# The delta rule's triangular inverse on TensorE: 128x128 products at every level, or 64x64 products on the halves and one joining block

## The reference, cut to what matters

```
kk = jnp.einsum('bnhik,bnhjk->bnhij', k, k)
a_low = jnp.where(strict, kk * decay * beta[..., :, None], 0.0)
rhs = jnp.concatenate([v * beta[..., None], k * (beta * jnp.exp(gc))[..., None]], axis=-1)
uw = lax.linalg.triangular_solve(a_low + jnp.eye(C, dtype=a_low.dtype), rhs,
                                 left_side=True, lower=True, unit_diagonal=True)
...
    v_new = u_i - jnp.einsum('bhck,bhkv->bhcv', w_i, S)
    o_i = jnp.einsum('bhck,bhkv->bhcv', q_i, S) + jnp.einsum('bhij,bhjv->bhiv', qk_i, v_new)
    S = S * gl_i[..., None, None] + jnp.einsum('bhck,bhcv->bhkv', k_i, v_new)
```

## Time and profile before

| | us |
|---|---|
| median of 3 runs (lowest, highest) | 1306.34 (1304.51, 1308.42) |
| span of the profiled execution | 1308.6 |
| TensorE busy in it | 1204.4 |
| VectorE busy in it | 824.2 |
| ScalarE busy in it | 614.4 |
| delta stage's rounds 4 to 22 in it, about | 925 to 1082 |

### The profile page before, as it was taken

The page is one execution under the profiler, slowest core; times in us unless marked ns, Lnnn a source line. Parts: engine busy times, 40 slices in busy tenths (PEclk is TensorE's granted clock), DMA queues, the critical chain, the costliest instruction groups (busy, mean ns, idle before and its releaser), DMA issues.

```text
span 1308.6 us, 19807 instructions
## 1 busy us (share of the span) xinstructions
PE 1204.4 (92%) x8111; PEld 1070.4 (82%) x8111; DVE 824.2 (63%) x1298; ACT 614.4 (47%) x1097; POOL 63.9 (5%) x93
## 2 busy tenths in 40 slices
PE   2878999999999999889999999996789999999997
PEld 1757966788989889878999998995668887899996
DVE  7576574579998685557755447748665545544444
ACT  0431354564454455565455455365643334645543
POOL 0011055300000000000000000110000000000000
PEclk9989899999999999889999999898589999999999
DMA  9788502259999655323885651440000015456640
GB/s 351 277 294 297 196 28 65 97 181 350 365 348 339 218 167 171 116 78 118 284 272 184 215 181 37 135 153 1 1 1 17 1 65 177 134 190 192 193 162 33
DMA packets 138490, 218.76 MB, mean 167 GB/s; under 512 B 7056, under 2 KB 95504, under 8 KB 138016
## 3 DMA queue, kind: packets, MB, share of 16 engines
q1 hardware_dynamic: 138400, 217.49, 49.5%
HBM read 216.42 MB, written 1.05 MB: 166 GB/s over the span
## 4 chain that ended last, share of the span: by engine, by line
PE 78%; DVE 12%; ACT 5%; DMA 2%; issue 1%; POOL 1%; SPq 0%; DVEq 0%; ACTq 0%
PE bank L468 19%; PE bank L470 19%; PE bank L469 19%; PE bank L2146 2%; PE bank L2158 2%; PE bank L2154 2%; PE bank L493 2%; DVE ada_acc L537 1%; DMA ring<-ada_w 1%; PE bank L2406 1%; DMA ring<-ev_w_in 1%; DVE low L462 1%; DVE act_low L1335 1%; PE bank L1002 1%; PE bank L1037 1%
## 5 line engine op out<-in xcount | busy, mean ns | idle before, releaser
L462 DVE TENSOR_TENSOR low<-ring,high 128x2048 fp32r<-128x2048 f32 (+1 forms) x139 | 317.7, 2287 | 255.4 <-ACT high L456 254.8
L456 ACT ACTIVATE high<-ring 128x2048 fp32r<-128x2048 f32 (+1 forms) x139 | 264.5, 1905 | 262.0 <-PE bank L470 173.8
L468 PE MATMUL bank<-act_high,high 128*128 128x256 f32 (+1 forms) x1112 | 321.7, 289 | 6.0 <-DVE act_low L1335 6.0
L470 PE MATMUL bank<-act_high,low 128*128 128x256 f32 (+1 forms) x1112 | 316.4, 285 | 0.0
L469 PE MATMUL bank<-act_low,high 128*128 128x256 f32 (+1 forms) x1112 | 316.4, 285 | 0.0
L468 PE MATMUL bank<-high,act_high 128*128 128x512 f32 (+1 forms) x632 | 232.7, 368 | 2.5 <-DVE act_low L2651 1.8
L470 PE MATMUL bank<-high,act_low 128*128 128x512 f32 (+1 forms) x632 | 230.7, 365 | 0.0
L469 PE MATMUL bank<-low,act_high 128*128 128x512 f32 (+1 forms) x632 | 230.6, 365 | 0.0
L468 PEld LDWEIGHTS bank<-act_high,high 128*128 128x128 f32 x1112 | 214.0, 192 | 11.4 <-DVE act_low L1335 6.8
L469 PEld LDWEIGHTS bank<-act_low,high 128*128 128x128 f32 x1112 | 214.1, 193 | 2.6 <-issue 1.7
L470 PEld LDWEIGHTS bank<-act_high,low 128*128 128x128 f32 x1112 | 214.0, 192 | 0.0
(11 more groups left out here) (467 smaller groups left out, 1502.2 us busy)
## 6 DMA issues: line engine op xcount, KB each, us to landing
ring<-mlp_w SPq DMA_DIRECT2D x64, 1024.0 KB, 5.9
ring<-ada_w SPq DMA_DIRECT2D x48, 1024.0 KB, 7.2
ring<-w_up SPq DMA_DIRECT2D x16, 1024.0 KB, 5.6
ring<-w_down SPq DMA_DIRECT2D x16, 1024.0 KB, 4.9
ring<-od_w_in SPq DMA_DIRECT2D x12, 1024.0 KB, 5.2
ring<-w_in SPq DMA_DIRECT2D x11, 1024.0 KB, 5.3
ring<-ev_w_in SPq DMA_DIRECT2D x8, 1024.0 KB, 7.4
ring<-ev_w_out SPq DMA_DIRECT2D x4, 1024.0 KB, 8.3
```

The source lines that it names most:

```text
L456: e.activation(weights(c)[0], in_ring(("w", c)), ACT.Copy).then_inc(*act.up("high", c))
L462: e.tensor_tensor(low, in_ring(("w", c)), high.bitcast(F32), ALU.subtract).then_inc(*vec.up("low", c))
L468: e.matmul(out_, ah, bh, start=start, stop=False)
L470: return e.matmul(out_, al, bh, start=False, stop=stop)
```

## The change

For real chunks, X and XT of levels 0 to 5 are kept as their two 64x64 blocks on the diagonal, one on each half of the partitions, side by side in one buffer `xs` of eight groups (four heads of X, four of XT). A level's products are made as two 64x64 products a head, on the rows and columns of the array that belong to the half; X's and XT's updates go to one bank and are subtracted in one operation. At the level before the last, XT's blocks are written into a full 128x128 buffer, whose other corner was set to zero at the start. The last level makes the joining block alone: one 64x64 product a head from near rows to far columns, a copy, one product back, and a copy with a sign. Masks of the levels shrink to 64 columns, and one DMA of them with them. Meta chunks use the same buffers with their 16 rows whole. The order of steps, rounds and chunks is unchanged.

```diff
@@ square_masks
+    j = i // HALF * HALF + np.arange(HALF)[None, :]
     for back in (0, 1):
-        for level in range(LEVELS):
+        for level in range(JOIN):
...
+        def by_half(b, rows, n, at=0, groups=4):
+            return b[rows, at:at + groups * HALF].rearrange("p (g c) -> p g c", g=groups)[:, :, 0:n]
+
+        def halves_of(k, B, C, real, back):
+
+            if not real:
+                return (slice(0, C),), None, None, B["x"][0:C], B["w"][0:C, :, 0:C]
+            x = B["x"].rearrange("p a b -> p (a b)").rearrange("p (g c) -> p g c", g=8)
+            w = B["w"].rearrange("p a b -> p (a b)")[:, 0:4 * HALF].rearrange("p (g c) -> p g c", g=4)
+            return HALVES, HALVES[back], HALVES[1 - back], x, w
@@ delta_tensor
                 e.wait_ge(*vec.at("x", k, l - 1))
-                for h, o in enumerate(four(b)):
-                    m = e.matmul(o, B["aT"][0:C, h, 0:C], B["x"][0:C, h, 0:C], start=True, stop=True)
+                for h in range(4):
+                    if l == JOIN:
+                        m = e.matmul(b[far, at(h)], B["aT"][near, h, far], xs[near, h, :], start=True, stop=True)
+                    else:
+                        for r in parts:
+                            m = e.matmul(b[r, at(h)], B["aT"][r, h, r], xs[r, h, :], start=True, stop=True)
                 m.then_inc(*pe.up("w", k, l))
                 yield
                 e.wait_ge(*vec.at("w", k, l))
                 e.wait_ge(*vec.at("xT", k, l - 1))
-                if l < n_levels - 1:
-                    b = ps.take(e, ("x", k, l), vec, "x", k, l)
-                    for h, o in enumerate(four(b)):
-                        m = e.matmul(o, B["xT"][0:C, h, 0:C], B["w"][0:C, h, 0:C], start=True, stop=True)
-                    m.then_inc(*pe.up("x", k, l))
                 b = ps.take(e, ("xT", k, l), vec, "xT", k, l)
-                for h, o in enumerate(four(b)):
-                    m = e.matmul(o, B["w"][0:C, h, 0:C], B["xT"][0:C, h, 0:C], start=True, stop=True)
+                for h in range(4):
+                    if l == JOIN:
+                        m = e.matmul(b[near, at(h)], ws[far, h, :], B["xT"][far, h, far], start=True, stop=True)
+                        continue
+                    if l < n_levels - 1:
+                        for r in parts:
+                            e.matmul(b[r, at(h)], xs[r, 4 + h, :], ws[r, h, :], start=True, stop=True)
+                    for r in parts:
+                        m = e.matmul(b[r, at(4 + h)], ws[r, h, :], xs[r, 4 + h, :], start=True, stop=True)
                 m.then_inc(*pe.up("xT", k, l))
@@ delta_vector
-            e.tensor_tensor(v_("x"), v_("a"), level(0, 1 - back), ALU.mult).then_inc(*vec.up("x0", k))
+            for r in parts:
+                e.tensor_tensor(xs[r, 0:4, :], B["a"][r, :, r], level(0, 1 - back, r), ALU.mult).then_inc(*vec.up())
+            if real:
+                e.memset(B["xT"][far, :, near], 0.0).then_inc(*vec.up())
...
-            e.tensor_tensor(v_("xT"), v_("aT"), level(0, back), ALU.mult).then_inc(*vec.up("xT0", k))
+            for r in parts:
+                e.tensor_tensor(xs[r, 4:8, :], B["aT"][r, :, r], level(0, back, r), ALU.mult).then_inc(*vec.up())
+            vec.also("x0", k)
             e.wait_ge(*vec.at("x0", k))
-            e.tensor_tensor(v_("x"), idn, v_("x"), ALU.subtract).then_inc(*vec.up("x", k, 0))
-            e.wait_ge(*vec.at("xT0", k))
-            e.tensor_tensor(v_("xT"), idn, v_("xT"), ALU.subtract).then_inc(*vec.up("xT", k, 0))
+            e.tensor_tensor(xs, half_masks[0:C, 2 * JOIN, 0:N].unsqueeze(1).broadcast_to([C, 8, N]), xs, ALU.subtract).then_inc(
+                *vec.up("x", k, 0))
+            vec.also("xT", k, 0)
             for l in range(1, n_levels):
+                b = ps.of(("w", k, l))
                 e.wait_ge(*pe.at("w", k, l))
-                e.tensor_tensor(v_("w"), by_head(ps.of(("w", k, l)), C), level(l, 1 - back), ALU.mult).then_inc(*vec.up("w", k, l))
+                if l == JOIN:
+                    e.tensor_copy(ws[far], by_half(b, far, N)).then_inc(*vec.up("w", k, l))
+                else:
+                    e.tensor_tensor(ws, by_half(b, slice(0, C), N), level(l, 1 - back, slice(0, C)), ALU.mult).then_inc(*vec.up("w", k, l))
...
-                e.tensor_tensor(v_("xT"), v_("xT"), by_head(ps.of(("xT", k, l)), C), ALU.subtract).then_inc(*vec.up("xT", k, l))
+                if l == JOIN:
+                    e.tensor_scalar(B["xT"][near, :, far], by_half(b, near, N), -1.0, None, ALU.mult).then_inc(*vec.up("xT", k, l))
+                elif l == JOIN - 1:
+                    e.tensor_tensor(xs[near, 0:4, :], xs[near, 0:4, :], by_half(b, near, N), ALU.subtract).then_inc(*vec.up("x", k, l))
+                    for r in parts:
+                        e.tensor_tensor(B["xT"][r, :, r], xs[r, 4:8, :], by_half(b, r, N, 4 * HALF), ALU.subtract).then_inc(*vec.up())
+                    vec.also("xT", k, l)
+                elif l == n_levels - 1:
...
+                else:
+                    e.tensor_tensor(xs, xs, by_half(b, slice(0, C), N, 0, 8), ALU.subtract).then_inc(*vec.up("x", k, l))
+                    vec.also("xT", k, l)
@@ late_loads
-            e.dma_start(masks.rearrange("p a b -> p (a b)"), I["square_masks"][:, :]).then_inc(*landed.up("late"))
+            e.dma_start(all_masks, I["square_masks"][:, :]).then_inc(*landed.up("late"))
```

More of the change, by code:

```diff
@@ L47 @@
 LEVELS = 7
+JOIN = LEVELS - 1
 ALL = slice(0, SEQ)
@@ L79, in square_masks @@
     blocks = [*incl, *[np.where(m, 0.0, -NEG) for m in strict], *[np.where(m, 0.0, NEG) for m in incl]]
+    j = i // HALF * HALF + np.arange(HALF)[None, :]
     for back in (0, 1):
-        for level in range(LEVELS):
+        for level in range(JOIN):
             b = 1 << level
-            joined = (i // (2 * b) == j // (2 * b)) & (i // b % 2 == 0) & (j // b % 2 == 1)
-            blocks.append(joined.T if back else joined)
+            even, odd = (j, i) if back else (i, j)
+            blocks.append((i // (2 * b) == j // (2 * b)) & (even // b % 2 == 0) & (odd // b % 2 == 1))
+    blocks.append(i == j)
     return np.concatenate(blocks, 1).astype(np.float32)
@@ L359, in program @@
         LATE = 9
-        masks = mem.take("masks", 6 + 2 * LEVELS, P, at=late_at)
+        all_masks = mem.take("masks", 6 * P + (2 * JOIN + 1) * HALF, at=late_at)
+        masks = all_masks[:, 0:6 * P].rearrange("p (a b) -> p a b", a=6)
+        half_masks = all_masks[:, 6 * P:].rearrange("p (a b) -> p a b", a=2 * JOIN + 1)
         after = late_at + (6 + 2 * LEVELS) * P
@@ L1756, in program @@
         meta_bufs = [{**{n: mem.take(f"d{d}_{n}_meta", 4, META, at=early_at[d] + 3 * 512 + i * 64)
-                         for i, n in enumerate(("a", "aT", "x", "xT", "w"))},
+                         for i, n in enumerate(("a", "aT", "w"))},
+                      "x": mem.take(f"d{d}_x_meta", 8, META, at=early_at[d] + 3 * 512 + 3 * 64),
                       "kdec": mem.take(f"d{d}_kdec_meta", 4, P, at=after + 336 + d * 512),
@@ L2109, in delta_tensor @@
             M1 = masks[0:C, back, 0:C]
+            parts, near, far, xs, ws = halves_of(k, B, C, real, back)
+            N = HALF if real else C
+            at = lambda h: slice(h * HALF, h * HALF + N)
             g = ba[0:C, t, 8 + 4 * d:12 + 4 * d]
@@ L2181, in delta_tensor @@
                 o = b[0:C, tok(h)]
-                m = e.matmul(o, B["xT"][0:C, h, 0:C], B["bv"][0:C, h, :], start=True, stop=not real)
+                m = e.matmul(o, B["xT"][:, h, :] if real else xs[:, 4 + h, :], B["bv"][0:C, h, :], start=True, stop=not real)
                 if real:
@@ L2277, in delta_vector @@
             beta = ba[0:C, t, 4 * d:4 * d + 4]
-            idn = wide(ident[0:C, 0:C])
-            level = lambda l, back_: wide(masks[0:C, 6 + LEVELS * back_ + l, 0:C])
+            parts, near, far, xs, ws = halves_of(k, B, C, real, back)
+            N = HALF if real else C
+            level = lambda l, back_, r: wide(half_masks[r, JOIN * back_ + l, 0:N])
             e.wait_ge(*act.at("e_tot_in", k))
@@ L2320, in delta_vector @@
                 yield
-                if l < n_levels - 1:
-                    e.wait_ge(*pe.at("x", k, l))
-                    e.tensor_tensor(v_("x"), v_("x"), by_head(ps.of(("x", k, l)), C), ALU.subtract).then_inc(*vec.up("x", k, l))
+                b = ps.of(("xT", k, l))
                 e.wait_ge(*pe.at("xT", k, l))
-                e.tensor_tensor(v_("xT"), v_("xT"), by_head(ps.of(("xT", k, l)), C), ALU.subtract).then_inc(*vec.up("xT", k, l))
+                if l == JOIN:
[6 more added lines that the diff above has]
+                elif l == n_levels - 1:
+                    e.tensor_tensor(xs[:, 4:8, :], xs[:, 4:8, :], by_half(b, slice(0, C), N, 4 * HALF), ALU.subtract).then_inc(
+                        *vec.up("xT", k, l))
+                else:
```

(2 more changed lines are left out.)

## The result

The changed kernel takes 1300.47 us, median of 16 runs (1281.44 to 1304.73), against 1306.61 (1303.13 to 1311.44, also 16). The forecast was 1280, its range 1270 to 1297. The 16 times fall into two groups with nothing between them: seven from 1281.4 to 1285.5 us (median 1284.3), with a mean TensorE clock over the span of 0.961 to 0.966, and nine from 1300.2 to 1304.7 us (median 1302.3), clock 0.946 to 0.950. The kernel before has one group. The ratio of the comparison, 0.984 [0.982, 0.987], counts eight of the nine upper runs as slow and leaves them out; the ratio of the plain medians is 1300.5 / 1306.6 = 0.995. So the forecast has two answers. By the ratio the time is 0.984 x 1306.3 = 1286 us, inside the range. The plain median lies 3.5 us above its upper end, and more than half of the executions are like that.

A forecast was written before the change was run, and what follows sets the result against it. TensorE was taken as the bound from round 9 on, with VectorE's queue setting part of the pace before. Gains along the path summed to 26.3 us: 1306.3 - 26.3 = 1280 us, range 1270 to 1297 (forecast's own 1271 to 1289).

The forecast's parts named there:

- The overlap: Levels 1 to 5: products on opposite halves run side by side in one bank, w 0.46 us, x and xT 0.91.
- switch: Change of tile shape between TensorE groups: 0.2 us each, 101 before and 117 after, 13 new ones in rounds 10 to 20.
- Rounds 4 to 8: Delta stage, 925.3 to 975.4 us: gains of 3.0, 0, 2.0 and 1.3 us, partly at the low clock; called the weakest term.
- the 16 operations of VectorE: Rounds 4 to 8, 943.9 to 952 us: these operations and their neighbours set the pace, so a gain of 0.
- Rounds 9 to 20: Delta stage from 975.4 us, TensorE always busy: 3.6 us gained in round 9, 16.4 in rounds 10 to 20.
- the last level's share: Last level of the chunks: 8 records on one tile for w and 8 for xT, 0.46 us each against 0.89.
- Rival 3, the clock: Lower clock holds on through rounds 9 to 20; decides from some 29 us more at the lower level; chance 0.04.
- its full form: Lower clock through all of rounds 9 to 20: about 60 us more, time near 1340 us, slower.
- The argument against rival 3: From 987.7 us on the grant is 1.00 in every stretch, and the new order leaves TensorE no gaps there either.
- Rival 2, another engine: Rounds 10 to 16: ScalarE's row operations or VectorE's waits take over, each round loses 1 us: 1288 to 1297; chance 0.06.

The follow-up runs named there:

- single file: Changed kernel with levels 1 to 5 done for all heads on the lower 64 partitions, then on the upper: 1351.5 us; with 16 unread products in round 8's wait 1341.1.
- fills of rounds 8 to 18: Changed kernel with unread 128x128 products in TensorE's waits: 16 in round 8, then 5 more, then 3 more in round 18: 1285.7, 1285.2, 1281.8 us.
- the kernel before with its fill: Kernel before with 16 unread 128x128 products in round 8's wait for x of chunk (0,1): 1304.15 us, ratio 0.9975.
- three fills: Changed kernel with 16 and 5 unread products in round 8's waits and 3 late ones before chunk (1,0)'s joining block, round 18: 1281.8 us, ratio 0.9815.
- the two filled kernels: Kernel before and changed kernel, each with 16 unread 128x128 products in round 8's wait for x of chunk (0,1): 1304.15 and 1285.7 us.
- all fills: Three fills plus 12, 3, 5 and 6 products in waits of rounds 4 and 5, zeroing moved: 1283.2 us; with 3 more in round 14, 1281.4.
- the last level alone: Kernel before with only its last level cut to the joining block: 1308.2 us, ratio 1.0010; with 3 unread products ahead of chunk (1,0)'s joining block 1305.5.
- the kernel with 12 products: Changed kernel, wait left unfilled, with 12 unread 128x128 products at the start of round 9, when the clock is already low: 1290.5 us.
- one or two fills of round 8: Changed kernel with 16 unread products in the wait of chunk (0,1), or also 5 in the wait of chunk (1,0): 1285.7 and 1285.2 us.

## Why the prediction was right where the clock came back, and too low for most executions

- **The overlap: right.** The groups cost 0.51 to 0.61 us (w) and 1.08 (pair, with switches), the forecast said 0.46 and 0.91 and 0.2 a switch; in single file the same groups cost 0.89 and 1.83, the bounds that the forecast had for it. Rounds 12 and 13 took 4.3 and 6.0 us (forecast 4.6 and 6.4). The rule of the Trainium skill (TensorEngine Tiling (Array Packing), Restrictions and Gotchas, PSUM Pressure), that different row tiles cannot access one bank simultaneously, does not hold for this pair of tiles, which write different partitions; the trace disagrees with 0.61 us for 16 records that need 0.89 in single file between the same neighbours.
- **Rounds 4 to 8: right in the sum, by luck.** 2.3 us up to the 16 operations of VectorE (943.73 against 946.05; forecast 3.0 and then 0), 2.1 to 964.24's mask, now at 959.80 (2.0), 1.8 to round 9 (1.3): 6.25 us, forecast 6.3. But not all of the 2.3 is the change's. From the first L2288 of the real chunks of round 0 (L2315 after; 908.85 and 908.33) to the 16 operations it is 37.1 to 37.2 us in all four traces with whole levels 1 to 5, and 35.4 to 35.5 in five of the six of the changed kernel and its fills of rounds 8 to 18 (36.2 in the other). So rounds 4 and 5 gave 1.7 us where the sum took 3.0, and the rest was there before them. The halves' maskings cost 0.43 each, not 0.33, and the zeroing took 0.30 of its 0 to 0.33; the two w groups at the low clock of round 8 gave more back, 1.05 us each where they took 1.73 and 1.97.
- **Rounds 9 to 20: right at full speed.** The fair pair are the kernel before with its fill and the kernel with three fills, both at a grant of 1.00 in round 9. Round 9 gains 3.6 us between them (11.06, 7.50; forecast 3.6), from round 10 to the last transposes it is 16.3 (86.30, 69.96), or 17.0 without the 3 late products; forecast 16.4. From the same first L2288 on, the stage is 24.7 us shorter, and 4.8 of it lie ahead of round 9; forecast 26.3 and 6.3. Within it the last level's share was mis-sized: 3.4 us by the forecast's own prices, 1.6 to 2.2 measured, since each of its 8 groups also pays a switch (0.60, not 0.46).
- **Rival 3, the clock: this is the step that failed in most executions.** It had a chance of 0.04 and the condition of 29 us more at the lower level. It came in 9 executions of 16 and 4 of 6; in the profiled one for 41 us (962 to 1003) where the kernel before had some 10 in rounds 8 and 9, and for 10 more at 1051: 41 us more, which meets the condition. It took 18 of the 26 us, not the 60 of its full form, since the clock did come back at 1003. The lower group, 1284.3, is 22.3 us faster than the kernel before, as the two filled kernels are by their medians (22.1): 4 us less than forecast. Of these 4 the traces show 1.3, in rounds 4 and 5. The argument against rival 3 was that TensorE has no gaps in these rounds. That was true, busy 11.70 of 11.70, 11.30 of 11.30, 13.30 of 13.30, and no protection: the clock stayed low all the same. The Trainium skill (TensorE: Matmul & The Clock Gate, Part 1: The HAM clock gate) has it that sustained busy work brings the full clock back; by that rule rounds 9 to 11 would take little more than the 21.5 us of three fills, and they took 36.3: the trace disagrees. The runs put this in the argument's place: the clock was back before 24 records on the whole array had ended (4.98 us), with work in pairs of halves it came back 34 us into busy rounds in one kernel and 3 to 7 us after a fall in three others, and with the single file order it stayed down for 77 us. Both orders let it fall with no wait near. That the change lowers what held the clock up, by taking whole-array products out, fits all of this and is argued from it; which property of the work decides is not shown. The forecast kept the kernel before's clock for a kernel whose work it had changed.
- **Rival 2, another engine: right as a mechanism, small by itself.** Waits of 0.33 us for `paT` in round 14, 0.55 for `d_w_last` in round 15 and 0.56 for `za` in round 19 are new. Their own price is 1.4 us; the last one costs about 4 to 5 when the clock falls behind it (3.9 us lost from round 19 on, 4.6 against three fills).

Open: what the clock does in the lower group (9 of 22 executions), of which no trace exists; why the same order of work gives both groups; why falls on the same kind of products last 3 to 7 us in some kernels and 41 in another; what quantity the chip looks at, since no run varied it alone; the 1.0 us behind the delta stage.

## What to carry to other kernels

Two products on different halves of the partitions overlap even into one PSUM bank, as long as neighbours in the order lie on different halves; order them so. When a change swaps 128x128 products for small ones, ask what holds TensorE's clock up afterwards: a busy share of 100% did not here, and part of the change's gain then hung on waits as short as 0.6 us. Look at single times, not the median alone: two groups with two mean clocks point to the cause before any trace is read, and a few products nobody reads in the wait ahead of such a stretch (here 24, in three places) are a cheap test and a cheap cure.

## What the runs showed of the hardware that was not expected

- TensorE at 1.2 GHz for 77 us while busy for all of them, in the kernel with the 64x64 products in single file (larger products of the attention and the chunks are among them); the fall came 13 us after its last wait. In the kernel with all fills, products in pairs, a fall came 14 us after the last wait and lasted 3 us.
- The same fp32 products in pairs of halves: 16 records in 0.61 us against 0.89 in single file between the same neighbours, 0.51 with another such group in front; one bank, disjoint partitions.
- A fall of the clock behind a wait of 0.56 us (in the changed kernel, with the last level alone, and in the kernel with 12 products) or 0.63 us, for 7 to 11 us; with one or two fills of round 8 the same wait of 0.56 us stood in the profile and no fall, so a short wait does not always bring one.
- VectorE takes 0.43 us for 64 partitions x 256 elements (operands in SBUF) and 0.42 for 128 x 256 with one operand in PSUM: in these two rows half the partitions save nothing.
